# Scaling the gated-delta values and keys by their gates inside the third level of the triangular inversion

## What is computed

```python
kb = k * beta[..., None]
L = jnp.where(strict, jnp.einsum("...id,...jd->...ij", kb, k) * decay, 0.0)
rhs = jnp.concatenate([v * beta[..., None], kb * jnp.exp(g)[..., None]], axis=-1)
sol = lax.linalg.triangular_solve(eye + L, rhs, left_side=True, lower=True, unit_diagonal=True)
u, w = sol[..., :dv], sol[..., dv:]
...
v_new = u_c - jnp.einsum("...cd,...de->...ce", w_c, S)
o = jnp.einsum("...cd,...de->...ce", q_c * jnp.exp(g_c)[..., None], S) + a_c @ v_new
k_w = k_c * jnp.exp(g_last - g_c)[..., None]
S = S * jnp.exp(g_last)[..., None] + jnp.einsum("...cd,...ce->...de", k_w, v_new)
```

## Time and profile before

| | |
|---|---|
| median of 3 runs | 3126.52 us (3124.45 to 3126.83) |
| profiled execution, its own time | 3130.82 us |
| its span | 3129.0 us |
| PE busy | 3034.8 us, 97% |
| DVE busy | 2018.4 us, 65% |
| ACT busy | 1593.5 us, 51% |
| POOL busy | 595.9 us, 19% |
| mean granted clock of PE | 0.988 |

### The profile page before, as it was taken

One profiled execution on the slowest core, in us unless ns is written; L12 is line 12 of the kernel. 1 busy time (PEld: TensorE's weight loads), 2 busy tenths in 40 slices (PEclk: granted clock), 3 DMA queues, 4 the chain that ended last, 5 costly groups with the idle time before them and its releaser, 6 DMA issues.

```text
span 3129.0 us, 55925 instructions
## 1 busy us (share of the span) xinstructions
PE 3034.8 (97%) x20655; PEld 2599.8 (83%) x20655; DVE 2018.4 (65%) x3332; ACT 1593.5 (51%) x2697; POOL 595.9 (19%) x502
## 2 busy tenths in 40 slices
PE   8999998999999999999999999989999999999998
PEld 7899887778888888888788998877788888888886
DVE  5775555776777777545568756557767777765554
ACT  5555653446555555444455556434465555544444
POOL 3000352440221222000000004533401222120000
PEclk9999998999999999999999999999999999999999
DMA  6666101115565656666556661021356656566654
GB/s 208 177 185 190 59 3 60 62 63 178 178 194 181 192 178 196 218 194 192 162 182 179 187 177 44 2 67 56 101 176 188 194 182 194 187 209 207 192 184 151
DMA packets 265226, 479.21 MB, mean 153 GB/s; under 512 B 17314, under 2 KB 81148, under 8 KB 264380
## 3 DMA queue, kind: packets, MB, share of 16 engines
q1 hardware_dynamic: 265020, 476.48, 49.1%
HBM read 474.32 MB, written 2.10 MB: 152 GB/s over the span
## 4 chain that ended last, share of the span: by engine, by line
PE 83%; issue 6%; DVE 4%; POOLq 2%; POOL 2%; ACT 1%; DVEq 1%; SPq 0%; DMA 0%; ACTq 0%
PE ps L665 82%; PE ps L669 1%; POOLq L555 1%; DVE wlo L1848 1%; DVE upair L1861 0%; POOLq L543 0%; DVE H L1880 0%; POOL KB L532 0%; POOL scores L464 0%; DVE TN L2278 0%; POOLq L566 0%; DVE XS L1898 0%; POOL KB L540 0%; POOL H L607 0%; ACT whi L1311 0%
## 5 line engine op out<-in xcount | busy, mean ns | idle before, releaser
L1848 DVE TENSOR_TENSOR wlo<-ring,whi 128x1024 fp32r<-128x1024 f32 (+4 forms) x909 | 1091.3, 1216 | 693.6 <-ACT whi L1311 686.7
L665 PE MATMUL ps<-upair,whi 128*128 128x512 f32 x4032 | 1414.5, 395 | 6.1 <-DVE upair L1861 5.5
L1311 ACT ACTIVATE whi<-ring 128x1024 fp32r<-128x1024 f32 (+4 forms) x947 | 940.7, 1003 | 801.7 <-PE ps L665 750.0
L665 PE MATMUL ps<-upair,wlo 128*128 128x256 f32 x4032 | 1131.0, 281 | 0.0
L665 PEld LDWEIGHTS ps<-upair,whi 128*128 128x128 f32 x4032 | 756.7, 188 | 184.1 <-issue 6.0
L665 PEld LDWEIGHTS ps<-upair,wlo 128*128 128x128 f32 x4032 | 762.7, 189 | 0.3 <-issue 0.2
L665 PE MATMUL ps<-whi,upair 128*128 128x390 f32 (+2 forms) x1280 | 367.5, 364 | 0.0
L647 POOL TENSOR_TENSOR YB<-YB 128x1024 f32<-128x1024 f32 x22 | 125.2, 5693 | 837.7 <-DVE YB L1871 837.7
L665 PE MATMUL ps<-whi,ghi 128*128 128x512 f32 x704 | 274.4, 390 | 0.0
L665 PE MATMUL ps<-whi,glo 128*128 128x512 f32 x704 | 274.0, 389 | 0.0
L665 PE MATMUL ps<-wlo,ghi 128*128 128x512 f32 x704 | 273.9, 389 | 0.0
(11 more groups left out here) (318 smaller groups left out, 3477.1 us busy)
## 6 DMA issues: line engine op xcount, KB each, us to landing
ring<-in_w_up_dram SPq DMA_DIRECT2D x352, 512.0 KB, 3.9
ring<-in_w_down_dram SPq DMA_DIRECT2D x176, 512.0 KB, 4.2
ring<-in_w_in_dram SPq DMA_DIRECT2D x128, 384.0 KB, 3.5
ring<-in_w_out_dram SPq DMA_DIRECT2D x64, 512.0 KB, 3.6
ring<-in_w_ple_gate_dram SPq DMA_DIRECT2D x64, 512.0 KB, 4.3
ring<-in_w_in_dram SPq DMA_DIRECT2D x51, 512.0 KB, 4.3
ring<-in_w_in_dram SPq DMA_DIRECT2D x64, 390.0 KB, 3.4
ring<-in_w_in_dram SPq DMA_DIRECT2D x32, 396.0 KB, 3.5
```

The source lines that it names most:

```text
L665: return pe.matmul(o_, a, b, start=start, stop=stop, skip_group_check=True)
L1311: return act.activation(o_, i_, f, **kw)
L1848: v.tensor_tensor(wlo[:, slot % RING, :, 0:w], ring[:, slot % RING, :, 0:w], whi[:, slot % RING, :, 0:w].bitcast(F32), SUB).then_inc(S["lo ...
```

## The change

Line numbers behind the change are a few higher. The scaled values go to a buffer of their own, `scaled_v`, laid over `sgate`, and the scaled keys to `scaled_k`, laid over `KB[0]`. The scaling becomes a function, `scaled_operands`, that `invert` calls (as `halfway`) in level 2, behind the two maskings and ahead of the two waits for the t products. It waits for Vt and OT and not for the last products of the inversion. The instructions are the same 14 (eight values, four keys, two gate products). PE and DVE read the new buffers.

```diff
+        scaled_v = [sgate[:, d, :].rearrange("p (u c) -> p u c", c=P) for d in range(2)]
+        scaled_k = [KB[0][:, d, :].rearrange("p (h c) -> p h c", c=P) for d in range(2)]
...
                         pe.wait_ge(S["gd_rhs"], n2 + (d + 1))
                         for h in range(2):
-                            last = mm(ps[4 * d][:, h * P:(h + 1) * P], TT[d][:, 2 * h + F, :], TN[d][:, 2 * h + F, :], True, True)
+                            last = mm(ps[4 * d][:, h * P:(h + 1) * P], TT[d][:, 2 * h + F, :], scaled_v[d][:, 2 * h + F, :], True, True)
...
-                            last = mm(ps[4 * d + 2][:, h * P:(h + 1) * P], XS[d][:, h, :], ufg[d][:, h, :], True, True)
+                            last = mm(ps[4 * d + 2][:, h * P:(h + 1) * P], scaled_k[d][:, h, :], ufg[d][:, h, :], True, True)
...
-            def invert(m2, between=None, before_last=None):
+            def invert(m2, between=None, before_last=None, halfway=None):
...
+                    if halfway and lv == 2:
+                        halfway()
...
-                    invert(m2, lambda lv: lv and ml_pair(i, n, n2, lv), products)
-
-                    v.wait_ge(S["gd_vtc"], n + 1)
-                    v.wait_ge(S["gd_ktc"], n + 1)
-                    for d in range(2):
-                        F = FIRST[d]
-                        v.wait_ge(S["inv_t"], m2 * LEV + (2 * LEV - 1 + d))
-                        for h in range(2):
-                            for t in range(NT):
-                                v.tensor_scalar(TN[d][:, 2 * h + t, :], Vt[:, 2 * h + t, :], pair_gates(i, 20 + 2 * t + d, h), None, MUL)
-                            v.tensor_scalar(XS[d][:, h, :], OT[:, 2 * h + F, :], pair_gates(i, 16 + 2 * F + d, h), None, MUL)
+                    def scaled_operands():
+                        v.wait_ge(S["gd_vtc"], n + 1)
+                        v.wait_ge(S["gd_ktc"], n + 1)
                         own_pair = slice(2 * i, 2 * i + 2)
-                        v.scalar_tensor_tensor(gflat[:, 4 + d:8 + d:2, own_pair], gflat[:, 20 + d:24:2, own_pair], -1.0,
-                                               gflat[:, 12 + d:16:2, own_pair], MUL, MUL)\
-                            .then_inc(S["gd_rhs"], 1)
+                        for d in range(2):
+                            F = FIRST[d]
+                            for h in range(2):
+                                for t in range(NT):
+                                    v.tensor_scalar(scaled_v[d][:, 2 * h + t, :], Vt[:, 2 * h + t, :],
+                                                    pair_gates(i, 20 + 2 * t + d, h), None, MUL)
+                                v.tensor_scalar(scaled_k[d][:, h, :], OT[:, 2 * h + F, :], pair_gates(i, 16 + 2 * F + d, h), None, MUL)
+                            v.scalar_tensor_tensor(gflat[:, 4 + d:8 + d:2, own_pair], gflat[:, 20 + d:24:2, own_pair], -1.0,
+                                                   gflat[:, 12 + d:16:2, own_pair], MUL, MUL).then_inc(S["gd_rhs"], 1)
+
+                    invert(m2, lambda lv: lv and ml_pair(i, n, n2, lv), products, scaled_operands)
+
...
                             v.scalar_tensor_tensor(rf[d][:, h, :], ps[4 * d + 2][:, h * P:(h + 1) * P], pair_gates(i, 4 + 2 * B + d, h),
-                                                   TN[d][:, 2 * h + B, :], MUL, ADD)
+                                                   scaled_v[d][:, 2 * h + B, :], MUL, ADD)
```

## The result

The changed kernel takes 3137.88 us (median of 7 runs, 3133.82 to 3146.78) where the kernel before takes 3126.52 (median of 7 as well, 3123.70 to 3134.55). The ratio is 1.0038, with a 95% interval from 1.0027 to 1.0048: slower by some 12 us. The forecast was 3123.5 us, its range ended at 3131. The profiled execution of after took 3142.71 us, with a span of 3141.0.

What follows compares the result with a forecast made beforehand. PE was taken as the bound, waiting 7.6 us for the scaling. Gain 8.7 us, less 3 x 1.7 and 0.1, gave -3.5, or -1.9 with another pair at 1.7; -3 was taken: 3123.5 us, range 3116.5 to 3131.

Steps and rivals of the forecast that it cites:

- The tail's gain: End of each pair: without the scaling block PE's next group starts 1.4 us earlier; 8.7 us gained over six pairs.
- What was named as late next: End of a pair, once the scaling is gone: PE's own work and ACT's copy become what is late.
- Pair 1: Level 2 of each layer's first pair, POOL idle: the added block costs PE 0 to 0.1 us.
- DVE gets in at the end of POOL's current instruction, and keeps POOL out as long as its own instructions follow closely: Level 2 of POOL-busy pairs: block waits for one split, then runs through; POOL's later split and masks 2.4 us late.
- the 1.7 us: Loss per POOL-busy pair, taken for three pairs: late masks delay DVE's weighting and so PE's products of level 4.
- If POOL gets in once inside the block, the pair loses about 2.3 us: Level 2 of POOL-busy pairs: variant losing 2.3 instead of 1.7 us a pair; sum -1, inside the forecast.
- the third pair of layer 0: PE's low clock there nearly hides POOL's delay: 0.1 us lost, or 1.7 at the full clock.
- POOL keeps DVE out: Rival, 15%: in level 2 of POOL-busy pairs the block waits until POOL's gapless chain ends; +9.8 us, 3136.3.
- a scaling several us long: Sign in the changed profile, level 2 of POOL-busy pairs, that the rival "POOL keeps DVE out" holds.
- No collision: Rival, 17%: POOL's instructions run beside the scalings; only the gain and the first pairs' small loss stay, -8.7 us, 3117.8.

## Why the prediction was wrong

- **The tail's gain: right, somewhat small.** 1.4 us a pair was forecast, 1.67 came (B -2.24, C +0.57). What was named as late next, PE's own state products and ACT's copy, is what DVE now waits for.
- **Pair 1: right.** No loss where POOL idles.
- **The step that failed** is "DVE gets in at the end of POOL's current instruction, and keeps POOL out as long as its own instructions follow closely". Its first half held: the first scaling took 0.4 us. Its second half was read from one place, three subtractions past a waiting POOL instruction, which the MLP's loop repeats 22 times, and doesn't hold here. POOL got in behind every scaling as long as it had something queued. So POOL's instructions kept their 2.37 to 2.39 us, where the addition was to take 4.7 to 4.9, and the scalings took 2.4 us each; the masks and the weighting, on which the 1.7 us were built, were not what PE waited for: it waited 2.6 us for the transposes, of whose delay the prediction let PE see 0.2. The trace of before had the contrary rows, behind the last pair: two subtractions of DVE and two additions of POOL, each ending a turn behind the other. They weren't read:

```profile
701.14 4.52 DVE L1848 TENSOR_TENSOR wlo<-ring,whi 128x1024 fp32r<-128x1024 f32 x2
```

```profile
701.38 3.20 POOL L607 TENSOR_TENSOR H<-H,partial 128x1024 f32<-128x1024 f32 x1 [23.80 <-DVE ylo L2223]
704.54 3.39 POOL L607 TENSOR_TENSOR H<-H,lnp 128x1024 f32<-128x1024 f32 x1
```

- **The case was even priced.** "If POOL gets in once inside the block, the pair loses about 2.3 us": it got in twice, which by the same working is 2.3 + 2.4 = 4.7 us, near the 4.2 that remain of 5.4 without the clock. The number of POOL instructions still queued at the block's start, two, stood in the earlier trace rows.
- **Left out: the clock behind the new wait**, about 1.2 us in each of the four pairs. And the third pair of layer 0, put at 0.1 or, at the full clock, at the full loss, lost as much as the others; its low clock in before was an event of that execution and not a property of the pair.
- **The rivals.** "POOL keeps DVE out" gave 3136.3, and by the prediction's own sign for it, a scaling several us long, it held. It is close to the time and not the mechanism: DVE wasn't kept out until POOL's chain ended, but held for one instruction at a time, and the chain happened to be two instructions long, so that its price is near by luck. "No collision" (3117.8) is what the run with the scaling in level 4 shows.

## What to carry to other kernels

Before work is moved onto an engine's idle time, count the instructions that GpSimd has queued there: while both engines have work of the kinds that met here, every such VectorE instruction may cost a whole GpSimd instruction, so many short ones, or even one tiny one, are as dear as a long one. The idle time is best taken where the other engine idles as well (here two levels later, 0.9961 of before), or on an engine that GpSimd's work didn't hold up (ScalarE, 0.9974). And a rule read from one place in another stage is to be looked for in all the places of the trace where the two engines meet.

## What the runs showed of the hardware

- DVE and POOL took turns one for one in every pair in which POOL had instructions queued, and with every form tried (a scaling of 128 columns, products of 128, 256 and 512, a gate product of 4). In the rows of these turns the instruction that started first went first (POOL's split at 598.11, the scaling at 598.17). Turns of 128 columns left POOL's instructions at 2.37 to 2.39 us, one of 512 made one 2.83 us long. Yet in the MLP the second and third of three subtractions passed a POOL instruction that had started before them. What decides between the two orders wasn't settled.
- DVE's maskings, which read a PE product, and ACT's scalings ran beside POOL's additions and splits at their own length (0.74 us for two maskings, 0.39 us a scaling).
- A wait of PE of 2.5 to 2.6 us was followed, in all four pairs of after, by 3.4 us at a granted clock near 0.5, which made two groups of small products 1.8 to 2.0 us long in place of 1.15.
